# Attention steps of a two-block transformer kernel: DVE's order in a step, and where four late modulation chunks are computed

## The reference, cut to what matters

```python
mod = silu(c) @ ada_w[1] + ada_b[1]                 # 6 x 1024: shift, scale, gate of attention and of MLP
h   = modulate(rms_norm(x, attn_norm[1]), sh_a, sc_a)
h_kv = modulate(rms_norm(x, kv_norm), sh_kv, sc_kv) # shared keys and values come from h_kv @ w_kv
q, gates = h @ w_in                                 # 16 heads of 64, 3 gates a head
o_c = softmax(q k_cmp) v_cmp                        # 15 compressed keys a group
o_s = softmax(q k_slc + bias) v_slc                 # with 256 tokens all four blocks are selected
o_w = softmax(q k_win + bias) v_win                 # the window covers all tokens
x = x + gt_a * ((g0 * o_c + g1 * o_s + g2 * o_w) @ w_out)
x = x + gt_m * squared_relu_mlp(modulate(rms_norm(x, mlp_norm[1]), sh_m, sc_m))
```

## Time and profile before

| | |
|---|---|
| median of 3 runs | 1546.38 us (1540.44 to 1551.09) |
| profiled execution | 1543.09 us, its span 1541.2 us |
| TensorE matmul busy | 1341.2 us (87%), mean granted clock 0.92 |
| VectorE (DVE) busy | 902.9 us (59%) |
| ScalarE (ACT) busy | 672.7 us (44%) |
| GpSimd (POOL) busy | 166.7 us (11%) |
| DMA | 267.38 MB, 173 GB/s over the span |

### The profile page before, as it was taken

One profiled execution on the slowest core, in us unless ns is written; L12 is line 12 of the kernel. 1 busy time (PEld: TensorE's weight loads), 2 busy tenths in 40 slices (PEclk: granted clock), 3 DMA queues, 4 the chain that ended last, 5 costly groups with the idle time before them and its releaser, 6 DMA issues.

```text
span 1541.2 us, 21718 instructions
## 1 busy us (share of the span) xinstructions
PE 1341.2 (87%) x8420; PEld 1149.2 (75%) x8420; DVE 902.9 (59%) x1498; ACT 672.7 (44%) x1118; POOL 166.7 (11%) x167
## 2 busy tenths in 40 slices
PE   5888889999699888799996649789999797789999
PEld 2778679888599555689984536679998686689998
DVE  2678588886745555864445563465555566354443
ACT  2355353435434443454443444254444455254442
POOL 0634010101000000011001020010100010010010
PEclk8899989999799889899997767889999899889999
DMA  9966559999266442395651330268655254246660
GB/s 352 306 215 224 150 179 330 318 310 315 82 177 208 137 137 66 98 314 176 191 180 49 123 82 1 69 141 275 175 177 179 90 182 110 82 137 192 194 187 29
DMA packets 248789, 267.38 MB, mean 173 GB/s; under 512 B 10992, under 2 KB 182768, under 8 KB 248304
## 3 DMA queue, kind: packets, MB, share of 16 engines
q1 hardware_dynamic: 246064, 263.52, 54.5%
q10 hardware_dynamic: 2624, 2.48, 0.5%
HBM read 264.82 MB, written 1.15 MB: 173 GB/s over the span
## 4 chain that ended last, share of the span: by engine, by line
PE 68%; DVE 14%; issue 6%; ACT 5%; DMA 5%; POOL 1%; ACTq 0%; SPq 0%; DVEq 0%
PE bank L495 14%; PE bank L497 13%; PE bank L496 13%; PE ps_s L495 3%; PE ps_s L496 3%; PE ps_s L497 3%; PE ps_p L496 3%; PE ps_p L495 3%; PE ps_p L497 3%; DVE wlo L1262 2%; DVE acc L1281 2%; DMA wring<-in_mlp_w 2%; ACT whi L2152 2%; DMA wring<-in_ada_w 1%; PE ps_s L579 1%
## 5 line engine op out<-in xcount | busy, mean ns | idle before, releaser
L1262 DVE TENSOR_TENSOR wlo<-wring,whi 128x1024 fp32r<-128x1024 f32 (+1 forms) x373 | 453.6, 1234 | 269.4 <-ACT whi L2152 265.7
L2152 ACT ACTIVATE whi<-wring 128x1024 fp32r<-128x1024 f32 (+1 forms) x373 | 389.1, 1051 | 396.2 <-PE bank L497 129.1
L495 PE MATMUL bank<-h_hi,whi 128*128 128x256 f32 x1216 | 353.8, 291 | 12.8 <-DVE h_lo L1356 11.2
L496 PE MATMUL bank<-h_lo,whi 128*128 128x256 f32 x1216 | 349.8, 288 | 0.0
L497 PE MATMUL bank<-h_hi,wlo 128*128 128x256 f32 x1216 | 349.5, 287 | 0.0
L495 PEld LDWEIGHTS bank<-h_hi,whi 128*128 128x128 f32 x1216 | 239.6, 197 | 19.1 <-DVE h_lo L1356 12.8
L496 PEld LDWEIGHTS bank<-h_lo,whi 128*128 128x128 f32 x1216 | 239.6, 197 | 0.7
L497 PEld LDWEIGHTS bank<-h_hi,wlo 128*128 128x128 f32 x1216 | 239.2, 197 | 0.0
L495 PE MATMUL bank<-whi,h_hi 128*128 128x512 f32 (+2 forms) x274 | 114.9, 419 | 44.0 <-DVE h_lo L1356 27.7
L2623 POOL TENSOR_TENSOR ex<-ex 128x512 f32<-128x512 f32 x64 | 71.2, 1112 | 631.5 <-ACT g_hi L2259 631.5
L1444 DVE TENSOR_TENSOR g_lo<-ex,g_hi 128x512 fp32r<-128x512 f32 x64 | 44.2, 691 | 131.2 <-POOL ex L2623 131.0
(11 more groups left out here) (336 smaller groups left out, 1881.1 us busy)
## 6 DMA issues: line engine op xcount, KB each, us to landing
wring<-in_mlp_w SPq DMA_DIRECT2D x128, 512.0 KB, 5.5
wring<-in_ada_w SPq DMA_DIRECT2D x96, 512.0 KB, 7.1
wring<-in_mlp_w_in SPq DMA_DIRECT2D x64, 512.0 KB, 4.7
wring<-in_mlp_w_out SPq DMA_DIRECT2D x64, 512.0 KB, 4.2
wring<-in_a_w_in SPq DMA_DIRECT2D x24, 512.0 KB, 6.0
wring<-in_moba_w_qkv SPq DMA_DIRECT2D x24, 512.0 KB, 4.3
wring<-in_kv_ada_w SPq DMA_DIRECT2D x16, 512.0 KB, 7.7
wring<-in_w_kv SPq DMA_DIRECT2D x12, 512.0 KB, 5.9
```

The costliest lines, as they stand in the source:

```text
L495: nc.tensor.matmul(out, lh, rh, start=first, stop=False)
L496: nc.tensor.matmul(out, lh, rl, start=False, stop=False)
L1262: v.tensor_tensor(piece_view(wlo, p), raw_view(p), piece_view(whi, p).bitcast(F32), ALU.subtract).then_inc(lo_ready, 1)
L2152: a.activation(piece_view(whi, p), raw_view(p), ACT.Copy).then_inc(hi_ready, 1)
```

## The change

- The loads of the first two late chunks move ahead of those of `w_kv`. Their rows are computed in the gap, one before each token tile's transposes, their columns after the second tile, their drains after the norm. `row_sums` has four buffers in place of two (two of them in `ex`), and ACT's `norm` takes a `beside`.
- The other two late chunks are computed in steps 4 to 7, two rows of tiles in each half step; their columns stand in steps 6 and 8, their sums in 5 and 7, their drains in 7 and 9.
- `cmp_scores(0)` stands ahead of `q_pair(2)`; the turn of the compressed weights moves from step 1 to 0 (ACT's copy with it), the gate rows to step 2, DVE's gate copies to step 3, `cmp_weigh(1)` from step 7 to 6.
- In each step DVE does `nsa_low` and `nsa_weigh(b)` before `nsa_copy(b-1)` and before the split.

```diff
-    plan += w_kv[:2] + cmp + w_kv[2:] + b_in[:1] + b_in[2:]
+    plan += ada(1, range(6, 8)) + w_kv[:2] + cmp + w_kv[2:] + b_in[:1] + b_in[2:]
...
-        plan += ada(1, range(6, 10)) if lo == 0 else []
+        plan += ada(1, range(8, 10)) if lo == 0 else []
...
-        row_sums = [xn[:, 1, i * W:(i + 1) * W] for i in range(2)]
+        row_sums = [ex[:, :, :].rearrange("p a c -> p (a c)")[:, i * W:(i + 1) * W] for i in range(2)]
+        row_sums += [xn[:, 1, i * W:(i + 1) * W] for i in range(2)]
...
+            def late_rows(i, k0=0, k1=KT):
+                key = late[i]
+                b = bank_take(pe, ("late_rows", i)) if k0 == 0 else uses["late_rows", i][0]
+                if i < 2:
+                    piece_of["late_rows", i] = -1
+                for k in range(k0, k1):
...
...
-            turn_both("kv", 2)
+            for t in range(TT):
+                late_rows(t)
+                pe.wait_ge(sem("normed"), TT * NORMS.index("kv") + t + 1)
+                turn("kv", t)
+            for t in range(TT):
+                late_columns(t)
+            turned("kv", TT - 1, 2)
...
+            cmp_scores(0)
             q_pair(2)
-            cmp_scores(0)
-            gate_rows("n1", 64 + 16)
...
                 elif b < 8:
-                    if i == 0:
-                        late_rows(b - 4)
-                    elif b > 4:
-                        late_columns(b - 5)
+                    late_rows(b // 2, 4 * (b % 2) + 2 * i, 4 * (b % 2) + 2 * i + 2)
...
-                if b == 1:
+                if b == 0:
                     cmp_turn(0)
+                if b == 2:
+                    gate_rows("n1", 64 + 16)
+                if b in (6, 8):
+                    late_columns(b // 2 - 1)
                 if b == 8:
-                    late_columns(3)
                     cmp_turn(1)
...
# DVE, after the norm "kv"
+            late_drain(0)
+            late_drain(1)
...
# DVE, the loop
-            gate("n1")
...
-                if 6 <= b < 10:
-                    late_drain(b - 6)
+                if b in (7, 9):
+                    late_drain((b - 3) // 2)
                 if b < 16:
                     nsa_scores(b)
+                if b >= 3 and b % 2:
+                    nsa_low((b - 3) // 2)
+                if b < 16:
+                    nsa_weigh(b)
+                if b == 3:
+                    gate("n1")
+                if b == 6:
+                    cmp_centre(1)
                 if 1 <= b <= 16:
                     nsa_copy(b - 1)
-                if b >= 3 and b % 2:
-                    nsa_low((b - 3) // 2)
+                if b == 6:
+                    cmp_weigh(1)
                 if b % 2 == 0 and (b < 4 or b >= 8):
                     keep_ahead("dve", p0 + (b // 2 if b < 4 else b // 2 - 2))
-                if b == 6:
-                    cmp_centre(1)
-                if b == 7:
-                    cmp_weigh(1)
-                if b < 16:
-                    nsa_weigh(b)
...
# ACT: the norm and the loop
-            def norm(name, outs, gains, ready=None, after=None, last=None):
+            def norm(name, outs, gains, ready=None, after=None, last=None, beside=None):
                 for t in range(TT):
                     x_squares(name, t, ready and ready[t], after and after(t))
                     if last is not None and (t == 0 or name == "o"):
                         keep_ahead("act", last - 2 + t)
+                    if beside and t == 0:
+                        beside(0)
                 if gains:
                     act.wait_ge(sem("gains_ready"), gains)
                 split_turned(name, 0, outs)
+                if beside:
+                    beside(1)
...
-                if b == 1:
+                if b == 0:
                     cmp_copy(0)
...
-                if 4 <= b < 8:
-                    late_sums(b - 4)
+                if b in (5, 7):
+                    late_sums((b - 1) // 2)
```

More of the change, by code:

```diff
@@ L642, in out_product, with late_columns @@
                 by_token((key, 1), (h_hi, h_lo), KT, apart=True)
+            def late_rows(i, k0=0, k1=KT):
[4 more added lines that the diff above has]
+                for k in range(k0, k1):
+                    load = load_of[key, k - k % 2, 0]
+                    if k % 2 == 0:
+                        load_wait(pe, load)
+                    r = 32 * (k % 4)
+                    last = nc.tensor.matmul(bank[r:r + 32, b, :], c_pad[:, k, :], loaded(load)[:, k % 2, :],
+                                            start=(k < 4), stop=(k >= 4), skip_group_check=True)
+                    if k % 2:
+                        freed[load] = (sem("late_half"), i + 1) if k < 4 else (filled[b], uses["late_rows", i][1])
+                    if k == 3:
+                        last.then_inc(sem("late_half"), 1)
+                if k1 == KT:
+                    last.then_inc(filled[b], 1)
+            def late_columns(i):
+                bank_emptied(pe, ("late_rows", i))
+                b = bank_take(pe, ("late_mod", i))
+                for j in range(4):
+                    last = nc.tensor.matmul(bank[:, b, j:j + 1], row_sums[i][:, j * P:(j + 1) * P], ones[:, 0:1],
+                                            start=True, stop=True)
+                last.then_inc(filled[b], 1)
             def lookup(s):
@@ L928, in o_part @@
                     piece_over(last)
[L930 to L955, removed]
             def cmp_scores(half):
@@ L1737, in _, with late_drain @@
                  lambda t: y_residual("m0", True, t), last_of(("m0_w2", 7)))
+            def late_drain(i):
+                key = ("late_mod", i)
+                src = bank_full(dve, key)
+                at = col["ada_b1"] + 24 + 4 * i
+                v.tensor_tensor(mod[:, 4 * (22 + i):4 * (23 + i)], src[:, 0:4], params[:, at:at + 4],
+                                ALU.add).then_inc(drained[uses[key][0]], 1)
+                bank_emptied(dve, key)
+                v.memset(stat[:, 1:2], 0.0).then_inc(mod_drained, 1)
+            late_drain(0)
+            late_drain(1)
             v.memset(blocks[:, :, :, :, NCMP:16].rearrange("p s l g n -> p (s l) (g n)"), 0.0)
@@ L1824, in cmp_weigh @@
                 ins.then_inc(sem("cmp_weights"), 1)
[L1826 to L1833, removed]
             def nsa_scores(b):
@@ L2355, in _, with late_sums @@
             mlp("m0")
+            def late_sums(i):
+                key = ("late_rows", i)
+                a.activation(row_sums[i], bank_full(act, key), ACT.Copy).then_inc(drained[uses[key][0]], 1)
             norm("kv", [(h_hi, h_lo, gs, mod[:, 64:72]), (hk_hi, hk_lo, gs2, mod[:, 48:56])], 4, ready=(6, 8),
-                 last=last_of(("m0_w2", 7)))
+                 last=last_of(("m0_w2", 7)), beside=late_sums)
             def nsa_kv(w):
@@ L2373, in q_drain @@
                 drain(("q", i), q_t[:, 2 * i:2 * i + 2, :].rearrange("p j t -> p (j t)"), (0, W), 0.125)
[L2375 to L2380, removed]
             def cmp_exp(half):
```

## The result

The changed kernel takes 1573.43 us (median of four runs, 1571.85 to 1575.91) against 1547.2 us: 1.0174 of the kernel before, 95% interval 1.0148 to 1.0200. It is slower, as forecast, but by 26 us where 14.2 were forecast, and 0.4 us outside the range. The profiled execution took 1572.48 us, its span is 1570.6 us. The two profiled executions differ by 29.4 us, the medians by 26.2; what follows is read from the profiled ones.

A forecast was written before the change was run, and what follows sets the result against it. No engine is full in the loop; a chain through TensorE, DVE and ACT bounds it. A longer chain (8.3 us) plus lower TensorE clock (5.9) gave 14.2, added to the median 1546.38: 1560.6 us, range 1543 to 1573.

The forecast's parts named there:

- the chain through DVE: Attention loop: DVE's copy queues behind the weighing, two chains become one; a late pair costs 13.61 us for 11.10.
- the lengths at full clock: Late loop steps at full TensorE clock: even 5.77 us, odd after a split 7.84 us.
- The sum for steps 0 and 1: Loop start: scores 0 at 493.0 us, three splits in step 0 (3.45 us), scores 2 on TensorE at 508.4.
- the clock term: TensorE's lower clock in the loop: a slow step costs 1.08 us, a third of 16 steps, 5.9 us; bounds 0 and 17.
- my working: Step-by-step loop lengths at full clock, such as 6.5 us for step 2 and 5.77 or 7.84 for steps 9 to 15.
- Its 8.3 us: Attention loop: it ends 8.3 us later if every TensorE step runs at full clock.
- The start of the loop: Compressed scores of half 0 move ahead of q pair 2, so scores 0 start 1.9 us earlier, at 493.0.
- The gap: Where the shared norm is made, 403 to 421 us: taken as zero, ends -2.5 and +0.8 us.
- Late chunks at nothing: Loop: 5.7 us of TensorE work leaves, but beside the DVE chain; taken as nothing, -5.7 us at best.
- The first: Loop: TensorE waits for the weighing and the copy is early enough; faster, 1533 us; chance 0.12.
- The second: Loop: longer chain with the clock full nearly throughout; +8.3 us, 1554.7 us; chance 0.28.
- The third: Loop: TensorE's waits put it at the lower clock level throughout; +25 us, 1572 us; chance 0.15.

The follow-up runs named there:

- experiment 4: Changed kernel plus seven float32 matmuls of a zero tile in TensorE's wait in each of steps 9, 11, 13 and 15: 1567.19 us, 1.0150 of before.
- Experiment 2: Kernel before with DVE's new order alone (low split, weighing, copy, weight split; second compressed weighing in step 6): 1571.61 us, 1.0173 of before.
- experiment 5: Kernel before with one edit, DVE's weight split moved behind the weighing: 1533.32 us, 0.9916 of before.
- the four pairs above: Kernels with and without the moved work: 1.0174 and 1.0173, 0.9923 and 0.9916, 0.9871 and 0.9869, and 0.9973 against the kernel before itself.
- experiment 6: Changed kernel with DVE's copy first and weight split last, and ACT's high split ahead of its copy in even steps: 1527.39 us, 0.9871 of before.
- experiment 7: Kernel before with DVE's weight split last and ACT's high split ahead of its copy, without the moved work: 1526.63 us, 0.9869 of before.
- experiment 1: Changed kernel with DVE's old order put back (copy, low split, weight split, weighing; second compressed weighing in step 7): 1541.90 us, 0.9973 of before.

## Why the prediction was right or wrong

**Right: the chain through DVE, and the lengths at full clock.** One chain through DVE in place of two, a copy that waits for four exponentials, an odd step held by the split ahead of its scores. Measured at full clock (experiment 4), 5.75 and 7.82. The sum for steps 0 and 1 was 15.4 us, 493.0 to 508.4; they took 15.12, with the three splits at 503.98 in one row (3.48 us) as forecast. Experiment 2 shows that the loss is this order and, to some 0.4%, nothing beside it.

**Wrong: the clock term**, 5.9 us of the 14.2. I priced a slow step at 1.08, by following the lower clock along DVE's chain, and gave it to a third of the steps (of 16 steps that is 5.8, a slip of 0.1). Both factors were too low. At the lower level an even step isn't bound by that chain: TensorE's own work fills it (busy 8.24 of 8.24), and it costs 2.47 more than at full clock, not 1.08. The row for it was in hand: step 10 of the kernel before, at the lower level, took 7.46 (563.60 to 571.06) where step 12 took 4.73. And it was not a third of the steps but every even one from 2 to 14.

Against my working the even steps 2 to 14 took, in turn, 2.4, 2.3, 2.1, 3.1, 1.9, 2.5 and 1.4 us more: 15.7. The odd steps 3 to 13 took 1.5 more, the end of the loop some 2.7. With -0.3 for the first two steps that is 19.6 in the profiled execution, where the clock term had 5.9 and, as its upper bound, 17.

That the clock makes this, and the wait before it the clock, is shown by experiment 4 for steps 12 and 14 (2.5 and 1.4 us). That the clock makes the excess of steps 2 to 8 is read from their windows (0.74, 0.60, 0.63 and 0.64) and wasn't tried. At the end of the loop the stretch after the wait of step 15 stood at 0.53 (629.36 to 635.00); with that wait filled in experiment 4, the scores of step 15 to the norm took 28.88 us in place of 30.25, 1.4 of the 2.7.

The sum had a second fault in the same term. Its 8.3 us set a new loop with every step at full clock against the kernel before as it ran, in which steps 6, 8 and 10 had lost 7.7 us at 0.60 to 0.67 (experiment 5). So the term had to hold the whole clock loss of the new loop, with what the old one had already, and 5.9 is less than those 7.7 alone. In steps 6 and 8 (9.21 and 9.43 us after the change) the clock was low before it too, so that the new waits can't be said to have brought it there.

**The start of the loop** came 0.8 us earlier after the norm and not 1.9: the compressed scores, moved ahead of q pair 2, ran at the lower level there (32 matmuls in 3.60 us at 0.50, 1.96 before at 1.00).

**The gap** cost nothing and gave almost nothing, as taken. The high split of `w_kv` 0 waited 3.30 us for its load and came 1.6 us later against the residual, which had 2.19 us of idle time ahead of it before and has 0.55 now. With the rows and columns TensorE was busy for 9.77 of the 18 us in place of 3.35, but its products with `w_kv` still began at the lower level (matmuls 0.41). The tenth of their triples started 5.22 us after the first, 5.75 before: some 0.5 of the 0 to 2.5 us that might have come back did.

**Late chunks at nothing**: right by the four pairs above, each to some 0.4%. In steps 4 to 7 alone, where they are, experiment 6 took 22.2 us and experiment 7 27.1, but at different clocks. Experiment 5 has the kernel before's work in these steps with all four at 1.00, as experiment 6 has the moved work, and neither has a weight split there: 24.1 and 22.2. So at equal clock the move gives 1.9 us in steps 4 to 7 of single executions, and not the 5.7 of TensorE's work that left the loop. The rows say why, in the main. These lines of the changed kernel are a quarter of a chunk in step 7 and what follows it:

```profile
557.85 1.05 PE L656 MATMUL bank<-wring,pos_f 128*32 128x512 f32 x4
558.83 0.55 PE L1016 MATMUL ps_p<-ident,ex 128*128 128x128 f32 x3
```

and these a whole chunk in step 7 of the kernel before, also at 1.00:

```profile
543.35 1.92 PE L939 MATMUL bank<-wring,pos_f 128*32 128x512 f32 x16
545.20 0.55 PE L1007 MATMUL ps_p<-ident,ex 128*128 128x128 f32 x3
```

A quarter, which writes two of the four strips, takes 0.98 from start to start, a chunk so 3.9, close to the 3.8 that the prediction named and within its 1.9 to 4.7; whole it takes 1.85. The two chunks that stay cost 4.1 us more of TensorE's time, so that 1.6 of the 5.7 is left.

**Rivals.** The first (the weighing is what TensorE waits for) fell: the wait for `ex` did go, and the wait for the copy took its place and more. The second (clock full nearly throughout) fell. The third came nearest, 1572 us. Its mechanism, long waits of TensorE that pull the clock down, is the one that experiment 4 shows for the late steps; its number is partly luck, since it had every step slow at 1.08 each, and it was half of them at some 2.2 (15.7 over seven). I gave it 0.15 on the argument that 570 to 606 of the kernel before kept its clock with TensorE 79% busy; but its waits there were 1.2 us, and the new ones are 3.7.

## What to carry to other kernels

When an operation is moved ahead of another on an in-order engine, ask what it waits for and who waits for the one that is now behind it; in this loop an operation with an early input (the copy) belonged ahead of one with a late input (the weighing), and work that nobody waits for yet (the weight split) behind both. Price a lower TensorE clock by TensorE's own work in the step and not along the chain of another engine, since the bound changes with the clock. A new idle time of some microseconds on TensorE in a loop can cost twice, once as the wait and again in the work that follows it. And when a sum sets a new loop at full clock against an old one as it ran, the old one's clock loss must be added back.

## What the runs showed of the hardware that was not expected

How regularly the clock followed the wait in the late steps: in the changed kernel steps 9, 11 and 13, with an idle time of 4.2, 3.7 and 3.7 us on TensorE, are followed by steps at 0.55, 0.50 and 0.62 granted clock. Matmuls of zeros were enough to hold it: the filler multiplied a tile of zeros, and the stretch of steps 11 and 12 stood at 1.00.

A long wait is not the only thing that goes with a low clock. Waits of 1.2 and 0.9 us in each odd step of the kernel before left 570 to 606 at 1.00; waits of the same 1.2 and 0.9 in step 11 of experiment 1 were followed by step 12 at 0.61. And it fell with no idle time to speak of in the profile. In the kernel before, TensorE was busy for all of step 5 (7.67 us) and of step 6, which stood at 0.67. In the changed kernel it came down as the compressed scores began, behind 6.4 us without a gap:

```profile
480.00:486.40 6.40, 6.40 (x59) 6.40 (x57) 2.07 (x2) 1.75 (x3) 0.00 (x0) 0.99 0.78 251
486.40:490.03 3.63, 3.63 (x33) 3.54 (x33) 0.96 (x2) 1.16 (x2) 0.00 (x0) 0.50 0.23 83
```

Why it fell there no run tells.
